# The gate stage of a hybrid GLA and short-convolution layer, computed over pairs of 512-token blocks

## The chip, the cores and the metric

The kernel runs on one core of a Trainium2 chip. Five engines work side by side, each with an instruction queue of its own: PE (TensorE) multiplies matrices, DVE (VectorE) and ACT (ScalarE) work elementwise, POOL (GpSimd) does slower elementwise work and issues DMAs, SP (SyncE) issues DMAs. They meet at semaphores. The metric is the time of one execution in microseconds of device time (us).

## The reference

```python
n   = RMSNorm(h)
z   = n @ W_in
A   : GLA group (chunk-causal state readout, per-head RMSNorm, SiLU gate path)
B   : short gated conv group, SiLU gate path
h   = h + W_out [A ; B]
h   = h + sigmoid(h W_g + b_g) * (p[i] W_ple)
Final RMSNorm.
```

The sequence has 4096 tokens, h has 1024 channels, p has 256, and everything is float32. The change is in the last two lines: the product h W_g (1024x1024), the sigmoid, the small product p W_ple (256x1024), the sum into h, and the final norm over 1024 channels.

## The kernel before

Tokens lie along the free axis in 8 blocks of 512 (TB), channels along the 128 partitions in 8 tiles (KT). The first stage (eight `gla` blocks, to about 645 us) makes the GLA half. Then come 12 steps over pairs of blocks: 8 `conv` steps and 4 `out_proj` steps (g = 0 to 11), about 76.5 us each, and last the gate stage.

Each of these stages multiplies by a scheme with 7 products in place of 8 (P1, P6, P7, P2, P5, P3, P4, in this order, `OPERAND`): the tokens and the channels are halved, a product takes a quadrant (4 tiles of 128 channels by half of the tokens) or a sum or difference of quadrants (t1 to t4), and each product has 4 output tiles q. P1, P6, P7, P4 accumulate in one set of PSUM banks (A), P2, P5, P3 in another (C); between them ACT copies intermediate sums to SBUF (EA, EB). For float32 accuracy every operand is split in a high part (ACT writes XH) and a low part (DVE writes XL), and each tile takes three products: WH XH, WL XH, WH XL. One tile is therefore 4 x 3 = 12 matmuls, one product 48, one round of seven 336.

In the 12 steps a round covers a pair of blocks, so a quadrant has 512 columns. In the gate stage a round covers one block, so a quadrant has 256 columns (HT), and two tiles q share a PSUM bank. There, for each block b, `gate_product` runs the seven products from the weight tile WC, in which all seven weights (2 MB each) lie for the whole stage. The block's h lies in `raw` or `raw_odd`, both operand and residual, and DVE makes t1 to t4 from it (TA, TB_). `ple_unit` makes p W_ple for two tiles at a time, 12 matmuls of 256 columns for each, 96 for a block. `gate_sum` (DVE) adds the PSUM result to a copy, `sigmoid` (ACT) follows, `gate_mix` (DVE, two instructions: multiply by the PSUM result of `ple_unit`, add to the residual), `gate_square` (ACT) squares h, and `add_square` (DVE) sums the squares. The sum over channels is a product with a matrix of ones (`out_stats` on PE), then Ln and Exp on ACT (`out_rms`), and 8 scaled multiplies on DVE (`final_norm`). These engines wait for each other in the order in which each `gate` function lists its calls; there is no scheduler. SP loads the next block's h and p and stores the result; POOL does nothing in the gate stage.

In the 12 steps POOL makes the differences t3 and t1 (L921) and loads the quadrants of the next step into RQ, `block_hi` and `block_lo` split them, and POOL prepares the weights of the next stage, those of the gate too (`strip`, `gate_parts`, `prep_tile`).

## Time and profile before

| what | us |
|---|---|
| three runs | 2001.92, 2003.32, 2003.65 |
| median | 2003.32 |
| span of the profiled execution | 2000.1 |
| gate stage in it, first to last matmul of its rounds | 1569.9 to 1987.6 |
| from there to the end | 12.5 |

The profile holds one execution. Its span is counted from the first instruction to the last; what the device adds around it is not recorded apart, so its own time is known only as this span, which is 3.2 us under the median of the three runs.

### The profile page before, as it was taken

How to read it: one execution, taken by the hardware profiler on the slowest of the kernel's cores; microseconds unless marked ns; L12 is line 12 of the kernel's file. 1: busy time of each engine (PE TensorE's matmuls, PEld its weight loads, DVE VectorE, ACT ScalarE, POOL GpSimd, SP SyncE). 2: the span in 40 equal slices, each digit the busy share in tenths (PEclk: the TensorE clock that was granted, in tenths of full speed). 3: DMA queues.
4: the chain of work that ended last, by engine and by line, in shares of the span. 5: the costliest groups of instructions: out<-in, count | busy, mean ns of one | idle time of the engine just before them, and what ended most of it. 6: DMA issues, size and time to landing. Idle time of an engine off the chain costs nothing.

```text
span 2000.1 us, 28931 instructions
## 1 busy us (share of the span) xinstructions
PE 1973.4 (99%) x11280; PEld 1720.0 (86%) x11280; DVE 1346.4 (67%) x1574; ACT 780.5 (39%) x1221; POOL 692.8 (35%) x758
## 2 busy tenths in 40 slices
PE   6999999999999999999999999999999999999998
PEld 5888888888888888888888888888887999999998
DVE  6766666767644586685685685675575577777776
ACT  5444354444433533232332332323223254455544
POOL 4766656767661132332222221154652000000000
PEclk9999999999999999999999999999999999999999
DMA  6345445354448322237422227585586912222222
GB/s 239 131 167 201 152 161 204 121 194 172 164 163 322 141 95 95 85 107 295 158 88 90 69 95 290 181 301 197 182 301 235 378 68 92 82 87 77 95 96 85
DMA packets 89905, 322.84 MB, mean 161 GB/s; under 512 B 11664, under 2 KB 24384, under 8 KB 78784
## 3 DMA queue, kind: packets, MB, share of 16 engines
q1 hardware_dynamic: 56928, 185.46, 25.5%
q0 software_dynamic: 32864, 135.85, 18.8%
q8 instruction: 74, 1.21, 0.2%
q14 instruction: 39, 0.32, 0.0%
HBM read 193.34 MB, written 127.93 MB: 161 GB/s over the span
## 4 chain that ended last, share of the span: by engine, by line
PE 93%; DVE 3%; issue 1%; ACT 1%; DMA 1%; POOLq 0%; POOL 0%; SPq 0%; DVEq 0%; ACTq 0%
PE bank L1285 14%; PE bank L1291 14%; PE bank L1287 14%; PE bank L994 8%; PE bank L998 8%; PE bank L995 8%; PE bank L1373 5%; PE bank L1371 5%; PE bank L1376 4%; PE bank L1424 2%; PE bank L1423 2%; PE bank L1422 2%; PE bank L1381 1%; PE bank L1119 1%; PE bank L1179 1%
## 5 line engine op out<-in xcount | busy, mean ns | idle before, releaser
L1285 PE MATMUL bank<-XH,WC 128*128 128x512 f32 x1344 | 524.6, 390 | 1.9 <-DVE xt L2285 1.5
L1291 PE MATMUL bank<-XL,WC 128*128 128x512 f32 x1344 | 522.9, 389 | 0.0
L1287 PE MATMUL bank<-XH,WC 128*128 128x512 f32 x1344 | 522.9, 389 | 0.0
L2119 DVE TENSOR_TENSOR XL<-RQ,XH 128x1024 fp32r<-128x1024 f32 x168 | 220.3, 1345 | 218.3 <-ACT XH L1687 216.9
L1285 PEld LDWEIGHTS bank<-XH,WC 128*128 128x128 f32 x1344 | 252.3, 188 | 54.7 <-DVE xt L2285 1.9
L1291 PEld LDWEIGHTS bank<-XL,WC 128*128 128x128 f32 x1344 | 252.3, 188 | 52.5
L1287 PEld LDWEIGHTS bank<-XH,WC 128*128 128x128 f32 x1344 | 252.3, 188 | 51.7
L1373 PE MATMUL bank<-XHg,WC 128*128 128x256 f32 x896 | 246.2, 283 | 0.0
L1371 PE MATMUL bank<-XHg,WC 128*128 128x256 f32 x896 | 246.2, 283 | 0.0
L1687 ACT ACTIVATE XH<-RQ 128x1024 fp32r<-128x1024 f32 x168 | 170.7, 1053 | 168.3 <-PE bank L1291 149.8
L1376 PE MATMUL bank<-XLg,WC 128*128 128x256 f32 x672 | 190.2, 283 | 0.0
L921 POOL TENSOR_TENSOR RQ<-RQ 128x1024 f32<-128x1024 f32 x48 | 116.8, 2456 | 179.3 <-DVE RQ L2138 167.3
L1373 PEld LDWEIGHTS bank<-XHg,WC 128*128 128x128 f32 x896 | 171.9, 192 | 0.4
L1371 PEld LDWEIGHTS bank<-XHg,WC 128*128 128x128 f32 x896 | 171.9, 192 | 0.3
L994 PE MATMUL bank<-XH,QG 128*128 128x512 f32 x384 | 152.5, 397 | 0.0
L998 PE MATMUL bank<-XL,QG 128*128 128x512 f32 x384 | 149.9, 390 | 0.0
L995 PE MATMUL bank<-XH,QG 128*128 128x512 f32 x384 | 149.6, 390 | 0.0
L1376 PEld LDWEIGHTS bank<-XLg,WC 128*128 128x128 f32 x672 | 129.0, 192 | 0.0
L1704 ACT ACTIVATE EA<-bank 128x512 f32<-128x512 f32 x96 | 57.3, 598 | 169.4 <-PE bank L1291 71.2
L766 POOL TENSOR_TENSOR PB<-PB,prep_hi 128x512 f32<-128x512 f32 x84 | 109.8, 1307 | 2.3
L909 POOL DMA_DIRECT2D RQ<-n_scratch x32 | 17.6, 549 | 201.3 <-issue 91.1
L994 PEld LDWEIGHTS bank<-XH,QG 128*128 128x128 f32 x384 | 72.1, 188 | 17.2 <-issue 2.8
(241 smaller groups left out, 3822.8 us busy)
## 6 DMA issues: line engine op xcount, KB each, us to landing
WC<-w_scratch SPq DMA_DIRECT2D x28, 2048.0 KB, 9.8
RQ<-n_scratch POOLq DMA_DIRECT2D x32, 1024.0 KB, 5.4
w_scratch<-prep_hi POOLq DMA_DIRECT2D x84, 256.0 KB, 2.3
w_scratch<-PB POOLq DMA_DIRECT2D x84, 256.0 KB, 2.3
n_scratch<-raw SPq DMA_DIRECT2D x8, 2048.0 KB, 7.3
y_scratch<-y_sb SPq DMA_DIRECT2D x64, 256.0 KB, 2.6
RQ<-y_scratch POOLq DMA_DIRECT2D x16, 1024.0 KB, 7.0
xt<-xb_dram SPq DMA_DIRECT2D x64, 256.0 KB, 4.9
```

The source lines that it names most:

```text
L921: pool.tensor_tensor(RQ[:, a, k], RQ[:, Q22, k], RQ[:, b, k], ALU.subtract).then_inc(made, 1)
L994: nc.tensor.matmul(acc_ap, hh[0], hh[1], start=(k == 0), stop=False)
L995: nc.tensor.matmul(acc_ap, lh[0], lh[1], start=False, stop=False)
L998: mm = nc.tensor.matmul(acc_ap, hl[0], hl[1], start=False, stop=(k == KT - 1))
L1285: nc.tensor.matmul(bank[:], WC[:, i, q, 0, k], xh, start=(k == 0 and i in (P1, P2, P5)), stop=False, skip_group_check=True)
L1287: nc.tensor.matmul(bank[:], WC[:, i, q, 1, k], xh, start=False, stop=False, skip_group_check=True)
L1291: mm = nc.tensor.matmul(bank[:], WC[:, i, q, 0, k], xl, start=False, stop=(k == 3), skip_group_check=True)
L1371: nc.tensor.matmul(acc_ap, WC[:, i, q, 0, k], xh, start=(k == 0 and q % 2 == 0 and i in (P1, P2, P5)), stop=False, skip_group_check=True)
L1373: nc.tensor.matmul(acc_ap, WC[:, i, q, 1, k], xh, start=False, stop=False, skip_group_check=True)
L1376: mm = nc.tensor.matmul(acc_ap, WC[:, i, q, 0, k], XLg[:, z % 2, k], start=False, stop=(k == 3), skip_group_check=True)
L1687: nc.scalar.activation(XH[:, slot(s) + 2 * h:slot(s) + 2 * h + 2], RQ[:, OPERAND[i], 2 * h:2 * h + 2], ACT.Copy).then_inc(sx_hi, 1)
L2119: nc.vector.tensor_tensor(XL[:, k], RQ[:, OPERAND[s % 7], 2 * h:2 * h + 2], XH[:, k].bitcast(F32), ALU.subtract).then_inc(sx_lo, 1)
```

## The change

The gate stage becomes four rounds over pairs of blocks (p = 0 to 3), written as further steps g = 12 to 15 of the same code as `out_proj`: quadrants of 512 columns in RQ, loaded from h_scratch and combined by POOL and DVE, split by `block_hi` and `block_lo` in halves. `product_tile` is one tile q. The pair is finished in 16 units of one tile and one channel tile each (`UNITS`), with 6 matmuls of 512 columns in `ple_unit`. The C sums of the gate use two banks (`C_RING`), the ple results two (`PLE_RING`), one unit per bank.

SBUF is laid out anew. Only three of the seven weight places remain (`RING`); product i is loaded again in every round, once product i-3 is done. The other four places hold the residual tiles (five groups of 1 MB, `res_near` and `res_far`, loaded from h_scratch a second time and stored as the result), p of both blocks, and the weights of `ple_unit`. `add_square` moves from DVE to POOL, the high part of the total (`total_out`) from DVE to ACT, and the sum of squares is kept for 512 tokens at a time, so that each round has two `out_stats` (t = 1, then t = 0), each with 8 `final_norm` instructions.

```diff
+RING = 3
+RES = 5
+PRODUCT = (P2, P5, P3, P4)
+UNITS = tuple([(0, q) for q in range(4)] + [(1, 0), (1, 1), (2, 0), (2, 1), (1, 2), (1, 3), (2, 2), (2, 3)]
+              + [(3, q) for q in range(4)])
+C_RING = (6, 3)
...
+            def stream_weights(p, i):
...
+                sp.wait_ge(sx_free, 4 * (7 * (STEPS + p) + i - RING + 1))
...
+                sp.dma_start(WC[:, gate_place(p, i)].bitcast(F32),
+                             w_scratch[3, i].rearrange("p (q h k c) -> p q h k c", q=4, h=2, k=4)).then_inc(w_chunk[i], 16)
...
+            def gate(p):
+                if p > 0:
+                    load_p(p, 0)
+                    store_out(4 * (p - 1) + 1, 16 * (p - 1) + 4)
+                    store_out(4 * (p - 1) + 2, 16 * (p - 1) + 8)
+                stream_weights(p, P2)
+                if p > 0:
+                    store_out(4 * (p - 1), 16 * (p - 1) + 12)
+                    store_out(4 * (p - 1) + 3, 16 * (p - 1) + 16)
+                stream_weights(p, P5)
+                if p > 0:
+                    load_res(4 * p + 2)
+                    load_res(4 * p + 3)
+                    load_res(4 * p + 1)
+                else:
...
+                load_res(4 * p + 4)
+                stream_weights(p, P3)
+                stream_weights(p, P4)
+                stream_weights(p, 7 + P1)
+                load_p(p + 1, 1)
+                stream_weights(p, 7 + P6)
+                stream_weights(p, 7 + P7)
...
+            def add_square(p, u):
...
+                pool.wait_ge(g_sq, 16 * p + u + 1)
+                if n > 0:
+                    pool.wait_ge(g_acc, n)
+                here = acc[:, RESULT[UNITS[u][0]][0]]
+                pool.tensor_tensor(here, here, square_tile(p, u), ALU.add).then_inc(g_acc, 1)
...
+            for p in range(NP):
+                g = STEPS + p
+                s = 7 * g
+                pool.wait_ge(rq_loaded[Q12], 16 * (g + 1))
+                pool.wait_ge(rq_loaded[Q22], 16 * (g + 1))
+                difference(g, Q12, Q12, t3_made)
+                if p > 0:
+                    add_squares(p - 1, range(8, 16))
+                split_waits(s + P6)
+                pool.wait_ge(t4_made, 2 * (g + 1))
+                difference(g, Q11, Q11, t1_made)
+                if p < NP - 1:
+                    for c in range(8):
+                        pool.wait_ge(rows_stored[c], 16 * 2 * (p + 2))
+                    split_waits(s + P7)
+                    load_quadrant(g + 1, Q12)
+                    split_waits(s + P5)
+                    load_quadrant(g + 1, Q11)
+                add_squares(p, range(4))
+                if p < NP - 1:
+                    split_waits(s + P3)
+                    pool.wait_ge(t1_made, 2 * (g + 1))
+                    load_quadrant(g + 1, Q22)
+                add_squares(p, range(4, 8))
+                if p < NP - 1:
+                    split_waits(s + P4)
+                    load_quadrant(g + 1, Q21)
+            add_squares(NP - 1, range(8, 12))
...
+            def wait_gate_bank(p, i, q):
...
+                elif i == P5 and q < 2:
+                    pe.wait_ge(g_sum, sums_to(p, 0, q + 2))
+                elif i == P5:
+                    pe.wait_ge(g_sum, sums_to(p, 2, q - 2))
+                else:
+                    pe.wait_ge(g_sum, sums_to(p, 1, q))
...
-            def gate(b):
-                gate_product(b, P1)
-                gate_product(b, P6)
-                if b > 0:
-                    out_stats(b - 1)
-                gate_product(b, P7)
-                for c, i in enumerate((P2, P5, P3)):
-                    gate_product(b, i)
-                    ple_unit(b, 2 * c)
-                    ple_unit(b, 2 * c + 1)
-                if b < NB - 1:
-                    gate_product(b, P4)
-                ple_unit(b, 6)
-                ple_unit(b, 7)
-                if b == NB - 1:
-                    gate_product(b, P4)
...
+            def out_stats(p, t):
+                n = 2 * p + 1 - t
+                pe.wait_ge(out_split, n + 1)
+                pe.wait_ge(g_sum, 12 * (p + 1))
+                mean_of_split(C_RING[1 - t], total_hi[:], total_lo[:]).then_inc(out_mean, 1)
...
+            def gate(p):
+                g = STEPS + p
+                def with_ple(c, q):
+                    product_tile(g, PRODUCT[c], q, None)
+                    ple_unit(p, c, q)
+                stage_of(g, P1, None)
+                product_tile(g, P6, 0, None)
+                if p > 0:
+                    out_stats(p - 1, 0)
+                for q in range(1, 4):
+                    product_tile(g, P6, q, None)
+                stage_of(g, P7, None)
+                for q in range(4):
+                    with_ple(0, q)
+                for two in range(2):
+                    for c in (1, 2):
+                        with_ple(c, 2 * two)
+                        with_ple(c, 2 * two + 1)
+                if p < NP - 1:
+                    for q in range(3):
+                        with_ple(3, q)
+                    out_stats(p, 1)
+                    with_ple(3, 3)
+                    return
+                ple_unit(p, 3, 0)
+                ple_unit(p, 3, 1)
+                product_tile(g, P4, 0, None)
+                product_tile(g, P4, 1, None)
+                out_stats(p, 1)
+                ple_unit(p, 3, 2)
+                product_tile(g, P4, 2, None)
+                ple_unit(p, 3, 3)
+                product_tile(g, P4, 3, None)
+                last_stats()
...
+            def total_out(p, t):
+                act.wait_ge(g_acc, added_to(p, 2 if t == 1 else 3))
...
+                nc.scalar.activation(total_hi[:], acc[:, t], ACT.Copy).then_inc(out_sum_hi, 1)
...
+            def gate(p):
...
+                if p > 0:
+                    sigmoid(p - 1, 15)
+                block_hi(s + 1)
+                if p > 0:
+                    gate_square(p - 1, 14)
+                copy_sum(g, P1, 0)
+                if p > 0:
+                    gate_square(p - 1, 15)
+                copy_sum(g, P1, 1)
+                if p > 0:
...
+                    out_rms(p - 1, 1)
+                copy_sum(g, P1, 2)
+                copy_sum(g, P1, 3)
+                block_hi(s + 2)
+                if p > 0:
+                    total_out(p - 1, 0)
+                copy_sum(g, P6, 0)
+                copy_sum(g, P6, 1)
+                if p > 0:
+                    out_rms(p - 1, 0)
+                copy_sum(g, P6, 2)
+                copy_sum(g, P6, 3)
+                block_hi(s + 3)
+                split_p_hi(p, 0)
+                split_p_hi(p, 1)
+                block_hi(s + 4)
+                for q in range(4):
+                    sigmoid(p, q)
+                    copy_sum(g, P7, q)
+                    if q > 0:
+                        gate_square(p, q - 1)
+                block_hi(s + 5)
+                gate_square(p, 3)
+                for u in range(4, 12):
+                    sigmoid(p, u)
+                    if u == 9:
+                        block_hi(s + 6)
+                    if u > 4:
+                        gate_square(p, u - 1)
+                block_hi(s + 7)
+                if p < NP - 1:
+                    sigmoid(p, 12)
+                    gate_square(p, 11)
+                    sigmoid(p, 13)
+                    total_out(p, 1)
...
+            def total_split(p, t):
+                dve.wait_ge(out_sum_hi, 2 * p + 2 - t)
+                nc.vector.tensor_tensor(total_lo[:], acc[:, t], total_hi[:].bitcast(F32), ALU.subtract).then_inc(
...
+            def gate(p):
...
+                else:
+                    gate_mix(p - 1, 14)
+                    block_lo(s + 1)
+                    gate_mix(p - 1, 15)
+                    final_norm(p - 1, 1)
+                block_lo(s + 2)
+                if p > 0:
+                    total_split(p - 1, 0)
+                    final_norm(p - 1, 0)
+                block_lo(s + 3)
+                make_t4(g)
+                split_p_lo(p, 0)
+                split_p_lo(p, 1)
+                block_lo(s + 4)
+                gate_sum(p, 0)
+                for u in range(1, 4):
+                    gate_sum(p, u)
+                    gate_mix(p, u - 1)
+                block_lo(s + 5)
+                gate_mix(p, 3)
+                gate_sum(p, 4)
+                for u in range(5, 12):
+                    gate_sum(p, u)
+                    if u == 9:
+                        block_lo(s + 6)
+                    gate_mix(p, u - 1)
+                block_lo(s + 7)
+                gate_mix(p, 11)
+                make_t2(g + 1)
+                if p < NP - 1:
+                    gate_mix(p, 12)
+                    total_split(p, 1)
+                    gate_mix(p, 13)
```

Three places in the order of instructions. The first is DVE where one round ends and the next begins. Before (one block to the next), with XLg the low part, acc and total the sum of squares, L2461 the final norm:

```order
L2392 TENSOR_TENSOR acc<-acc,osq 128x512 x2
L2400 TENSOR_TENSOR total<-acc 128x512
L2403 CAST total_hi<-total 128x512
L2405 TENSOR_TENSOR total_lo<-total,total_hi 128x512
L2358 TENSOR_TENSOR XLg<-TB__108,XHg 128x1024
L2358 TENSOR_TENSOR XLg<-TA,XHg 128x1024
L2349 TENSOR_TENSOR TA<-raw_odd,TB__108 128x1024
L2351 TENSOR_TENSOR TB__108<-raw_odd,TB__108 128x1024
L2358 TENSOR_TENSOR XLg<-raw_odd,XHg 128x1024
L2321 TENSOR_TENSOR PL<-p_raw,PH 128x1024
L2461 SCALAR_TENSOR_TENSOR raw<-raw,vec,R_out 128x512 x4
```

The same place now, with L2196 `block_lo`, L2413 and L2418 `gate_mix`, L2433 `final_norm`, L2423 `total_split`, L2215 `make_t4`, L2391 `split_p_lo`:

```order
L2196 TENSOR_TENSOR XL<-RQ,XH 128x1024 x2
L2413 TENSOR_TENSOR gt<-gt,bank 128x512
L2418 TENSOR_TENSOR res_near<-res_near,gt 128x512
L2433 SCALAR_TENSOR_TENSOR res_near<-res_near,vec,R_out 128x512 x8
L2196 TENSOR_TENSOR XL<-RQ,XH 128x1024 x2
L2423 TENSOR_TENSOR total_lo<-acc,total_hi 128x512
L2433 SCALAR_TENSOR_TENSOR res_near<-res_near,vec,R_out 128x512 x8
L2196 TENSOR_TENSOR XL<-RQ,XH 128x1024 x2
L2215 TENSOR_TENSOR RQ<-RQ 128x1024 x2
L2391 TENSOR_TENSOR PL<-p_raw,PH 128x1024 x2
```

Before, the low part of the total was made ahead of everything of the next block; now that of t = 0 stands behind eight norms of t = 1 and one `block_lo`.

The second place is ACT at the same point of the program now, with L1794 `copy_sum`, L1771 `block_hi`, L1901 and L1904 `out_rms`, L1894 `total_out`, L1887 `gate_square`:

```order
L1887 ACTIVATE osq<-res_near 128x512
L1794 ACTIVATE EA<-bank 128x512
L1925 ACT_TABLE_LOAD
L1901 ACTIVATE R_out<-bank,eps 128x512
L1904 ACTIVATE R_out<-R_out 128x512
L1794 ACTIVATE EA<-bank 128x512 x2
L1771 ACTIVATE XH<-RQ 128x1024 x2
L1894 ACTIVATE total_hi<-acc 128x512
L1794 ACTIVATE EB<-bank 128x512 x2
L1901 ACTIVATE R_out<-bank,eps 128x512
L1904 ACTIVATE R_out<-R_out 128x512
```

The high part of the t = 0 total stands behind all four copies of P1 and the high part of P7's operand.

The third place is DVE at units 9 to 11 of a round, where L2404 is `gate_sum`:

```order
L2404 TENSOR_TENSOR gt<-bank,EA 128x512
L2196 TENSOR_TENSOR XL<-RQ,XH 128x1024 x2
L2413 TENSOR_TENSOR gt<-gt,bank 128x512
L2418 TENSOR_TENSOR res_near<-res_near,gt 128x512
L2404 TENSOR_TENSOR gt<-bank,EB 128x512
L2413 TENSOR_TENSOR gt<-gt,bank 128x512
```

The low part of P4's operand (L2196) stands between the sum of unit 9 and the mix of unit 8, and the mix of unit 8 is what frees the PSUM bank for the `ple_unit` of unit 10.

## Rows read from the trace of the kernel before

**Rows 1.** The page: busy time, share of the span and instructions of each engine.
```profile
PE 1973.4 (99%) x11280; PEld 1720.0 (86%) x11280; DVE 1346.4 (67%) x1574; ACT 780.5 (39%) x1221; POOL 692.8 (35%) x758
```

**Rows 2.** Windows of the gate stage and of the end: length, busy by engine, clock, DMA.
```profile
1569.60:1987.60 418.00, 418.00 (x3472) 417.30 (x3471) 303.89 (x393) 206.93 (x328) 0.00 (x0) 1.00 0.28 106
1987.60:2000.10 12.50, 4.04 (x19) 2.92 (x17) 7.80 (x18) 4.77 (x9) 0.00 (x0) 0.83 0.51 168
```

**Rows 3.** Waits of PE from 640 to 1572: total, times, longest.
```profile
PE bank L1285 <- DVE xt L2285: 1.5, 1, 1.5
```

**Rows 4.** Timeline of PE: start, duration (us); matmuls of 512 columns, then of 256.
```profile
1289.99 0.39 PE L1285 MATMUL bank<-XH,WC 128*128 128x512 f32 x1
...
1299.51 0.39 PE L1285 MATMUL bank<-XH,WC 128*128 128x512 f32 x1
...
1702.08 0.28 PE L1376 MATMUL bank<-XLg,WC 128*128 128x256 f32 x1
...
1705.68 0.28 PE L1376 MATMUL bank<-XLg,WC 128*128 128x256 f32 x1
```

**Rows 5.** Timeline of PE and ACT where the first tile of a P1 ends.
```profile
1342.35 0.39 PE L1285 MATMUL bank<-XH,WC 128*128 128x512 f32 x1
...
1342.55 0.60 ACT L1704 ACTIVATE EA<-bank 128x512 f32<-128x512 f32 x1 [1.60 <-PE bank L1291]
```

**Rows 6.** Timeline of DVE: low parts, final norms, the first instruction of a mix.
```profile
1363.16 2.36 DVE L2119 TENSOR_TENSOR XL<-RQ,XH 128x1024 fp32r<-128x1024 f32 x2 [7.26 <-ACT XH L1687]
...
1642.45 2.73 DVE L2461 SCALAR_TENSOR_TENSOR raw<-raw,vec,R_out 128x512 f32<-128x512 f32 x4
...
1597.38 0.68 DVE L2379 TENSOR_TENSOR gt<-gt,bank 128x512 f32<-128x512 f32 x1
```

**Rows 7.** ACT: a timeline row of two high parts, then groups with mean ns.
```profile
1351.20 2.00 ACT L1687 ACTIVATE XH<-RQ 128x1024 fp32r<-128x1024 f32 x2
...
L1837 ACT ACTIVATE osq<-raw 128x512 f32<-128x512 f32 x24 | 15.2, 632 | 16.6 <-DVE raw L2383 16.6
...
L1850 ACT ACT_TABLE_LOAD x7 | 9.0, 1283 | 0.1
...
L1898 ACT ACTIVATE R_out<-bank,eps 128x512 f32<-128x512 f32 x7 | 4.8, 689 | 0.1
```

**Rows 8.** Timeline of DVE and POOL, 1397 to 1407, and one more POOL row.
```profile
1397.10 1.29 DVE L2273 TENSOR_TENSOR xt<-xt,EB 128x512 f32<-128x512 f32 x2
1399.46 5.17 DVE L2273 TENSOR_TENSOR xt<-xt,EB 128x512 f32<-128x512 f32 x2 [1.07 <-DMA xt<-xb_dram]
1404.55 2.47 DVE L2285 TENSOR_TENSOR xt<-xt,bank 128x512 f32<-128x512 f32 x4
...
1398.88 5.20 POOL L921 TENSOR_TENSOR RQ<-RQ 128x1024 f32<-128x1024 f32 x2 [0.60 <-DMA RQ<-y_scratch]
...
1360.93 1.30 POOL L766 TENSOR_TENSOR PB_late<-PB_late,hi_late 128x512 f32<-128x512 f32 x1
```

**Rows 9.** Timeline of SP and DVE in the last `out_proj` step (L511 weights of the gate).
```profile
1522.69 2.41 SPq L511 DMA_DIRECT2D WC<-w_scratch  x3
...
1545.39 0.69 DVE L2273 TENSOR_TENSOR xt<-xt,EA 128x512 f32<-128x512 f32 x1 [3.80 <-DMA xt<-xb_dram]
```

**Rows 10.** The end: matmuls with ones, last norms, a window where the clock changes.
```profile
1987.75 1.89 PE L1460 MATMUL bank<-acc,ones 128*128 128x256 f32 x8
...
1991.60 1.13 PE L1460 MATMUL bank<-osq,ones 128*128 128x256 f32 x4 [1.09 <-ACT osq L1837]
...
1991.06 6.42 DVE L2455 SCALAR_TENSOR_TENSOR raw_odd<-raw_odd,vec,R_out 128x256 f32<-128x256 f32 x16 [0.82 <-ACT R_out L1893]
...
1995.00:1996.00 1.00, 0.00 (x0) 0.00 (x0) 1.00 (x4) 0.00 (x0) 0.00 (x0) 0.95 1.00 327
```

**Rows 11.** The page's DMA issues (KB each, us to landing), and a busy window.
```profile
WC<-w_scratch SPq DMA_DIRECT2D x28, 2048.0 KB, 9.8
...
1530.00:1535.00 5.00, 5.00 (x23) 4.13 (x22) 3.80 (x7) 1.79 (x3) 0.00 (x0) 1.00 1.00 423
```

More of the change, by code:

```diff
@@ new lines, in product_tile @@
+                for k in range(4):
+                    if q == 0 and k % 2 == 0:
+                        pe.wait_ge(sx_hi, 2 * s + k // 2 + 1)
+                    xh, xl = XH[:, slot(s) + k], XL[:, slot(s) + k]
+                    nc.tensor.matmul(bank[:], WC[:, weights_of, q, 0, k], xh, start=(k == 0 and i in (P1, P2, P5)),
+                                     stop=False, skip_group_check=True)
+                    nc.tensor.matmul(bank[:], WC[:, weights_of, q, 1, k], xh, start=False, stop=False,
+                                     skip_group_check=True)
+                    if q == 0 and k % 2 == 0:
+                        pe.wait_ge(sx_lo, 2 * s + k // 2 + 1)
+                    mm = nc.tensor.matmul(bank[:], WC[:, weights_of, q, 0, k], xl, start=False, stop=(k == 3),
+                                          skip_group_check=True)
+                    if q == 3:
+                        mm.then_inc(sx_free, 1)
+                    elif k == 3:
+                        mm.then_inc(product_done, 1)
+                    if hook is not None:
+                        hook(16 * i + 4 * q + k)
@@ L1404, in ple_unit, with ple_tile @@
-            def ple_unit(b, u):
-                n = 8 * b + u
+            def ple_tile(t, m, acc_ap, tokens):
+                for k in range(PLE_K):
+                    nc.tensor.matmul(acc_ap, WPH[:, k, m], PH[:, t, k, tokens], start=(k == 0), stop=False)
+                    nc.tensor.matmul(acc_ap, WPL[:, k, m], PH[:, t, k, tokens], start=False, stop=False)
+                    mm = nc.tensor.matmul(acc_ap, WPH[:, k, m], PL[:, t, k, tokens], start=False,
+                                          stop=(k == PLE_K - 1))
+                return mm
@@ L1445, in out_stats @@
[L1445 to L1471 removed]
+                pe.wait_ge(p_lo, 2 * p + t + 1)
@@ L1478, in _ @@
                 step(g)
-            for b in range(NB):
-                gate(b)
-            last_stats()
+            for p in range(NP):
+                gate(p)
         @block.scalar
@@ L1943, in _ @@
                 step(g)
-            for b in range(NB):
-                gate(b)
+            for p in range(NP):
+                gate(p)
         @block.vector
@@ L2370, in gate_sum @@
-                other = EBg if u >= 4 else EAg
-                dve.wait_ge(g_copied, 6 * b + (1, 5, 3)[u // 2] + pair)
-                nc.vector.tensor_tensor(gt[:, n % 3], ps[GATE_C[pair]][:], other[:, pair], ALU.add).then_inc(g_sum, 1)
-            def gate_mix(b, u):
-                n = 8 * b + u
+                if n == 0:
+                    for c_ in range(8):
+                        dve.wait_ge(rows_stored[c_], 16 * 2 * NP)
+                wait_product(dve, 7 * g + PRODUCT[c], q)
+                dve.wait_ge(e_copied, 12 * g + (0, 8, 4)[c] + q + 1)
@@ L2450, in last_norm @@
[L2450 to L2463 removed]
+                wait_res(dve, p, c)
@@ L2517, in _ @@
                 out_proj(g)
-            for b in range(NB):
-                gate(b)
-            for n, t in enumerate((1, 0)):
-                dve.wait_ge(out_rstd, NB + n)
-                last_norm(t)
+            for p in range(NP):
+                gate(p)
 def kernel(x, p, norm_w, w_in, w_alpha_up, b_alpha, gla_norm_w, conv_w, conv_b,
```

714 lines of the change are left out of this document (263 added, 451 removed).

## The prediction

> **What bounds the kernel now.** I read the page first, and in it the busy shares: PE is busy for 99% of the span [rows 1]. Then the windows of the stages: in the gate stage PE is busy for all of its 418.0 us at clock 1.00, DVE for 303.9, ACT for 206.9, POOL for none [rows 2]. Then the waits of PE: between 640 and 1572 there is one of note, 1.5 us, for a DVE sum [rows 3]. So PE's own stream sets the time, and a change counts by how long PE takes for its matmuls and by each wait that it brings. The timeline of PE gives the price of a matmul, by the distance of their starts, since they overlap: 42 of 512 columns in 9.52 us, 0.2267 each; 30 of 256 columns in 3.60 us, 0.120 each [rows 4]. Two short ones cost 0.240, so 0.0133 us are paid for every pair that could be one.
>
> **PE's own work.** Before, a block has 336 + 96 matmuls of 256 columns, eight blocks 3456, with 14 of 512 columns for the statistics; that is 414.7 + 3.2 = 417.9 us, which is the 418.0 of the window. After, a round has 336 + 96 of 512 columns, four rounds 1728, or 391.7 us, and the statistics still take 7 x 2 matmuls. Gain: 23.0 us. Of the removed work on DVE (the sums of squares, the total) nothing counts by itself, as PE never waited for it.
>
> **The last step before the gate.** All three first weights of the gate, 6 MB, were issued together at 1522.7, because SP first waited for POOL's preparation of the ple weights; the xt tiles came late behind them (DVE waits 3.8 us for one), and that is where PE's 1.5 us lie [rows 3, 9]. Now this wait stands behind P4, the three loads go out one by one, and the 3 MB of residuals only after P5. I take the 1.5 us as gained.
>
> **The boundary of two rounds.** Let 0 be the start of P1 in a round p > 0. A tile takes 12 x 0.227 = 2.72 us, a product 10.88, a `ple_unit` 1.36, a unit 4.08, a statistic 0.45. PE comes to `out_stats(p-1, 0)` after P1 and one tile of P6, at 13.60. It waits for `total_split`. The chain behind it:
> - ACT sees a tile 0.2 us after PE has ended it [rows 5]. Copy P1 q1 runs 5.64 to 6.24 (0.60), then the table load of 1.28, Ln 0.69 and Exp, taken like the square of its size, 0.63 [rows 5, 7]: R_out for t = 1 at 8.9.
> - DVE then does eight norms at 0.68 (four in 2.73), to 14.3, and `block_lo` for P7, 2.36, to 16.7 [rows 6].
> - On ACT the copies of P1 end at 11.7, `block_hi` for P7 takes 2.0 to 13.7, `total_out` 0.6 to 14.3 [rows 5, 7]. It is there before DVE wants it.
> - `total_split` is one DVE instruction, about 0.65: done at 17.3, seen by PE at 17.4.
>
> So PE stands 3.8 us at each of three boundaries, 11.4 us. The floor is ACT's side alone, 14.3 + 0.7 = 15.0, or 1.4 a boundary. Queued behind it on PE are the rest of P6 and P7, and all engines wait for those. What is late next: Ln and Exp for t = 0 at about 22.8, eight norms to 28.2, `block_lo` for P2 to 30.5, `make_t4` to 32.8, while P2 starts at 36.9 (13.6 + 3.8 + 0.45 + 3 x 2.72 + 10.88); POOL's difference t1 (two of 2.4 to 2.6) to 38, P5's parts to 41.3, the first gate sum 41.9. PE's third tile of P2 wants that at 45.1. No further stall.
>
> **The low part inside unit 9.** Let 0 be the end of the product tile of unit 9. PE has 1.36 + 2.72 us of work and then wants the bank that the mix of unit 8 frees, at 4.08. DVE's sum ends at 0.9, ACT's sigmoid at 1.6 (one of 512 like the square, 0.63), its two high parts at 2.65 and 3.6, DVE's low parts at 3.9 and 4.85, the multiply of the mix at 5.5 (0.68; a whole mix is two such instructions, 1.36 at most) [rows 6, 7]. A stall of 1.5 us in each of four rounds, 6.0 us.
>
> **POOL beside DVE.** POOL was idle in this stage; now each round has four differences and 14 additions. At 1399 two DVE additions that read SBUF twice took 5.17 us instead of 1.29, as long as POOL's two differences beside them (5.20), while four that read a PSUM bank took 2.47 beside POOL, as ever [rows 8]. So the second instruction of a mix, the low parts and `make_t2` can each wait for a POOL instruction (1.30 for an addition, 2.6 for a difference), the sums and norms hardly. Where this falls between units it is hidden by 2 us of slack in a unit (4.08 against 0.68 + 1.36 on DVE). After unit 9 it is not: POOL gets P4's parts at 4.9, then does two differences to 10.4 and three late additions, while DVE has two mixes, the low part of the next P1, a mix and `make_t2`. Without contention `ple_unit` 13 has its bank 1.4 us early; with every one of these in the way I get 0.7 us late there and 0.7 at `ple_unit` 14, in three rounds. Bounds 0 and 4.5 us (8 if also the low parts in unit 3 are caught); I take 3.0, nearer the bound with contention, since the row shows full blocking. The Trainium skill (SBUF — State Buffer, Who interferes with whom) says that an instruction with two SBUF inputs and a GpSimd one that reads SBUF exclude each other, and that the first to start keeps the port for its whole length. By this rule the cost is the 4.5 and not less; the trace agrees with the exclusion, not surely with who wins.
>
> **The end.** Let E be the end of the last P4 tile. DVE has four norms of t = 1 until E + 1.6, the last mix until E + 2.9, ACT the square until E + 3.6. A matmul with ones in plain float32 is long: the eight records of 256 columns take 1.73 us from first to last start plus one, two for each matmul, so one of 512 columns takes 0.86 [rows 10]. Then Ln and Exp to E + 6.2, eight norms to E + 11.7, and the store about 2.6 (2000.1 less 1997.5) with its issue: E + 14.7 against 12.5 now [rows 2, 10]. Loss 2.2, and 0.3 for the ple units that stand before P4 in the last round.
>
> **Sum.** -23.0 - 1.5 + 11.4 + 6.0 + 3.0 + 2.2 + 0.3 = -1.6 us: a span of 1998.5 for 2000.1. The median of the runs stands 3.2 above the span, so 2001.7 us. That is inside the 0.2% (4 us) which a measurement of this kernel can tell from no change.
>
> **Edits costed at nothing.** The weights that are now reloaded: a product has two products' time, 21.8 us, and an issue lands in 9.8 [rows 11]. The tightest is P3: SP issues it after the norms of t = 0, the stores, P5 and the four residual loads. From 28.3 about 6 MB stand in the queue, P3 and two quadrants make 10; at the 0.42 MB per us of the busy window [rows 11] they are in at about 53, and P3 starts at 61.4. Without this cover each us more is a us of PE, three or four times. RQ, p and the residuals come earlier than this relative to use.
>
> **Rivals.**
> 1. *The waits are smaller and the gain stays* (faster). For it: PE waits almost nowhere now, and DVE and POOL have 27% or more idle in the stage. Against: the boundary chain has no slack in it. With the boundary at its floor of 1.4, contention 0 and the rest as above, 2003.3 - 23 - 1.5 + 4.2 + 6 + 2.5 = 1991.5; with no stall at all 1981.
> 2. *The clock drops at the boundaries* (slower). In the tail PE's last matmul ends at 1992.7, and the clock is 1.00 until about 1995.9, then 0.5, 1.2 GHz: the window 1995 to 1996 has 0.95 [rows 10]. It fell 3.2 us after PE's last work, and I foresee 3.8 us of idleness three times. From there each matmul costs up to double until the clock is back; bounds per drop are 0 and, if it lasts as long as the fall took, 2 to 3 us of PE time, so up to 9: 2011. The point from which it decides is a stall of about 3 us. The Trainium skill (TensorE: Matmul & The Clock Gate, Part 1) says that the throttled state is the default and activity releases it; by this rule a drop follows where the idleness is long enough; the trace agrees in its tail, and shows no wait of that length inside the stage.
> 3. *Weights or residuals late* (slower). If the queue moves at 0.25 MB per us, P3 comes at 28 + 40 = 68, 7 us late in three rounds: 2023. Against: the busy window moved 423 GB/s [rows 11].
> 4. *The matmuls of the new rounds are not at 0.227*. All 12 steps run the same code at this pace, so I leave it 1 in 50, within the range.
>
> **How the numbers follow.** The forecast, a net within 4 us, has 0.42. Rival 1 and sums below -4 have 0.32: the boundary or the contention need only be 2.4 us less than I say. Rival 2 0.12, rival 3 and stalls that I have not found 0.14. The likeliest case alone spans 1999.3 to 2007.3. For 8 in 10 I go down to 1991, rival 1, and up to 2011, rival 2. Faster by over 0.2% 0.33, within 0.42, slower 0.25.
>
> **What the profile after would show.** 3456 fewer matmuls of 256 columns and 1728 of 512 at 0.227; three PE waits of about 3.8 us on total_lo at the second tile of P6; four of 1.5 on gt before the ple matmuls of unit 10; smaller ones at units 13 and 14; the wait at 1546 gone; the last matmul of P4 14.7 before the end. I am wrong if DVE gets to `total_split` well before 17, if the clock shows 0.5 inside the stage, or if PE waits for a WC transfer.

## The result, and the profile after

The changed kernel takes 2015.1 us (median of 4 runs, 2012.4 to 2020.1) against 2003.5 for the kernel before (4 runs): ratio 1.0064, 95% interval 1.0053 to 1.0076. It is slower by 0.6%, clear of the noise, and outside the predicted range. Its profiled execution took 2013.6 us, its span is 2011.8 us where 1998.5 was forecast: 13.3 us to explain.

The page of the changed kernel, its busy line, answers to [rows 1]:

```profile
PE 1961.7 (98%) x9546; PEld 1632.0 (81%) x9546; DVE 1321.8 (66%) x1490; ACT 766.7 (38%) x1156; POOL 816.0 (41%) x842
```

1734 PE instructions are gone, the 1728 foreseen and six in the tail, and 512 columns still take 0.2267 us at full clock, yet the span is longer: the share of PE fell below 99%. So the waits come next. PE's waits from 1400 to 2030 (total, times, longest), which answer to [rows 3]:

```profile
PE bank L1115 <- DVE total_lo L2423: 10.5, 3, 3.5
PE bank L1485 <- DVE gt L2413: 9.0, 11, 1.6
PE bank L1390 <- DVE xt L2362: 3.4, 1, 3.4
```

The first two rows are the boundary (forecast 11.4) and units 9 to 14 (forecast 6.0 + 3.0). The third should have gone; it has more than doubled. The timeline of PE (start, duration) shows what waits do not:

```profile
1540.09 0.79 PE L1390 MATMUL bank<-XH,WC 128*128 128x512 f32 x1 [3.41 <-DVE xt L2362]
1540.68 0.63 PE L1392 MATMUL bank<-XH,WC 128*128 128x512 f32 x1
1541.11 0.63 PE L1396 MATMUL bank<-XL,WC 128*128 128x512 f32 x1
...
1694.45 0.50 PE L1115 MATMUL bank<-total_hi,ones 128*128 128x512 f32 x1 [3.49 <-DVE total_lo L2423]
1694.79 0.39 PE L1116 MATMUL bank<-total_lo,ones 128*128 128x512 f32 x1
...
1696.32 0.63 PE L1396 MATMUL bank<-XL,WC 128*128 128x512 f32 x1
1696.75 0.63 PE L1390 MATMUL bank<-XH,WC 128*128 128x512 f32 x1
...
1699.59 0.40 PE L1392 MATMUL bank<-XH,WC 128*128 128x512 f32 x1
```

Behind a wait of 3.4 or 3.5 us the starts stand 0.43 us apart instead of 0.23. That is the pace of half the clock, 1.2 GHz instead of 2.4. The windows (length, busy by engine, granted clock, DMA) say the same: two boundaries show it, the third does not. A clock of 0.5 inside the stage was one of the prediction's signs of being wrong.

```profile
1694.00:1700.00 6.00, 5.55 (x17) 4.43 (x18) 0.39 (x1) 0.45 (x1) 0.00 (x0) 0.72 1.05 395
1700.00:1706.00 6.00, 6.00 (x28) 4.91 (x28) 4.58 (x7) 2.91 (x6) 0.00 (x0) 1.00 0.22 94
1801.00:1806.00 5.00, 4.05 (x11) 3.23 (x12) 0.90 (x2) 0.00 (x0) 0.00 (x0) 0.66 1.03 369
1909.00:1915.00 6.00, 5.66 (x25) 4.71 (x26) 0.57 (x2) 1.81 (x3) 0.00 (x0) 1.00 1.01 380
```

The loss is read off the starts: 17 intervals from 1694.45 to 1700.06 take 5.61 us, 3.85 at 0.2267, so 1.8 us at a boundary where the clock fell; from 1540.09 to 1545.80 it is 5.71 for 13, so 2.8 us.

Why the wait for xt grew is read from what stands ahead of it: VectorE's low part of P5, which wants GpSimd's difference t1 (L971). Timelines of POOL, DVE and SP, changed kernel:

```profile
1515.79 0.56 POOL L913 DMA_DIRECT2D tile_raw<-w_ple_dram  x1 [7.23 <-DMA g_scratch<-tile_raw]
1524.52 1.04 POOL L915 TENSOR_SCALAR tile_hi<-tile_raw 128x1024 fp32r<-128x1024 f32 x1 [8.17 <-DMA tile_raw<-w_ple_dram]
...
1529.93 4.75 POOL L971 TENSOR_TENSOR RQ<-RQ 128x1024 f32<-128x1024 f32 x2
...
1533.46 3.57 DVE L2196 TENSOR_TENSOR XL<-RQ,XH 128x1024 fp32r<-128x1024 f32 x2 [12.29 <-ACT XH L1771]
...
1504.07 22.08 SPq L515 DMA_DIRECT2D WC<-w_scratch  x3
```

and of POOL in the kernel before, the same instructions:

```profile
1510.10 0.56 POOL L863 DMA_DIRECT2D tile_raw<-w_ple_dram  x1 [2.76 <-DMA g_scratch<-tile_raw]
1513.94 1.05 POOL L865 TENSOR_SCALAR tile_hi<-tile_raw 128x1024 fp32r<-128x1024 f32 x1 [3.28 <-DMA tile_raw<-w_ple_dram]
...
1522.49 4.75 POOL L921 TENSOR_TENSOR RQ<-RQ 128x1024 f32<-128x1024 f32 x2 [2.67 <-DVE RQ L2138]
```

SP now issues the gate's weights from 1504, not at 1522.7 [rows 9], while GpSimd prepares its two ple tiles one after the other. GpSimd's DMA waits grow from 2.76 and 3.28 us to 7.23 and 8.17, and t1, queued behind the second tile, starts 7.4 us later. That is the theory for the first miss; for the second it is that the falls of the clock follow from PE's idleness. The experiments test both, and the terms that held.

### The profile page after: what moved, and what is told of

Read it like the earlier page. It is cut to its first block, busy times and chain, and to the rows that moved or that the text cites. A ratio compares the mean times of both kernels' runs of the same rounds, so it can differ in the third digit from the quotient of the medians.

```text
span 2011.8 us, 25501 instructions
## 1 busy us (share of the span) xinstructions
PE 1961.7 (98%) x9546; PEld 1632.0 (81%) x9546; DVE 1321.8 (66%) x1490; ACT 766.7 (38%) x1156; POOL 816.0 (41%) x842
## 4 chain that ended last, share of the span: by engine, by line
PE 87%; DVE 6%; ACT 2%; issue 2%; DMA 2%; POOL 1%; DVEq 0%; SPq 0%; ACTq 0%; POOLq 0%
PE bank L1390 18%; PE bank L1396 18%; PE bank L1392 18%; PE bank L1088 8%; PE bank L1092 8%; PE bank L1089 8%; PE bank L1485 1%; DVE XL L2196 1%; PE bank L1487 1%; PE bank L1486 1%; PE bank L1213 1%; DVE res_near L2433 1%; PE bank L1273 1%; DVE XL L2030 1%; PE bank L1264 1%
## 5 line engine op out<-in xcount | busy, mean ns | idle before, releaser
L1390 PE MATMUL bank<-XH,WC 128*128 128x512 f32 x1792 | 701.1, 391 | 3.5 <-DVE xt L2362 3.4
L1392 PE MATMUL bank<-XH,WC 128*128 128x512 f32 x1792 | 699.3, 390 | 0.0
L1396 PE MATMUL bank<-XL,WC 128*128 128x512 f32 x1792 | 699.2, 390 | 0.0
L2196 DVE TENSOR_TENSOR XL<-RQ,XH 128x1024 fp32r<-128x1024 f32 x224 | 292.9, 1342 | 280.2 <-ACT XH L1771 278.7
L1390 PEld LDWEIGHTS bank<-XH,WC 128*128 128x128 f32 x1792 | 337.9, 189 | 74.2 <-DVE xt L2362 3.8
L1396 PEld LDWEIGHTS bank<-XL,WC 128*128 128x128 f32 x1792 | 337.6, 188 | 70.6
L1392 PEld LDWEIGHTS bank<-XH,WC 128*128 128x128 f32 x1792 | 337.8, 188 | 69.7
L1771 ACT ACTIVATE XH<-RQ 128x1024 fp32r<-128x1024 f32 x224 | 227.4, 1053 | 225.1 <-PE bank L1396 175.8
L971 POOL TENSOR_TENSOR RQ<-RQ 128x1024 f32<-128x1024 f32 x64 | 164.1, 2586 | 295.0 <-DVE RQ L2215 283.5
L1794 ACT ACTIVATE EA<-bank 128x512 f32<-128x512 f32 x128 | 76.1, 595 | 185.3 <-PE bank L1396 89.1
L1027 POOL TENSOR_TENSOR acc<-acc,osq 128x512 f32<-128x512 f32 x52 | 72.6, 1396 | 154.3 <-ACT osq L1887 153.3
L804 POOL TENSOR_TENSOR PB<-PB 128x512 f32<-128x512 f32 x48 | 63.3, 1319 | 64.3 <-issue 58.7
L1088 PEld LDWEIGHTS bank<-XH,QG 128*128 128x128 f32 x384 | 72.1, 188 | 17.2 <-issue 2.8
L1092 PEld LDWEIGHTS bank<-XL,QG 128*128 128x128 f32 x384 | 72.1, 188 | 15.8
L1089 PEld LDWEIGHTS bank<-XH,QG 128*128 128x128 f32 x384 | 72.2, 188 | 14.6
L1794 ACT ACTIVATE EB<-bank 128x512 f32<-128x512 f32 x64 | 38.2, 598 | 114.1 <-PE bank L1396 114.1
L1088 PE MATMUL bank<-VH,XH 128*128 128x512 f32 x192 | 76.8, 400 | 0.0
```

The lines of the kernel that those rows point to most:

```text
L971: pool.tensor_tensor(RQ[:, a, k], RQ[:, Q22, k], RQ[:, b, k], ALU.subtract).then_inc(made, 1)
L1027: pool.tensor_tensor(here, here, square_tile(p, u), ALU.add).then_inc(g_acc, 1)
L1088: nc.tensor.matmul(acc_ap, hh[0], hh[1], start=(k == 0), stop=False)
L1089: nc.tensor.matmul(acc_ap, lh[0], lh[1], start=False, stop=False)
L1092: mm = nc.tensor.matmul(acc_ap, hl[0], hl[1], start=False, stop=(k == KT - 1))
L1390: nc.tensor.matmul(bank[:], WC[:, weights_of, q, 0, k], xh, start=(k == 0 and i in (P1, P2, P5)), stop=False, skip_group_check=True)
```

## The experiments

All times are medians beside runs of the kernel before on the same chip (2002.7 to 2004.0).

**The last step, 1: early weights in the kernel before.** SP's wait for GpSimd's tiles is moved behind three weight loads and four stores, and the small load of p goes with it; nothing else changes.

```diff
-                if g == STEPS - 1:
-                    sp.wait_ge(tile_stored, 16 * 2 * (STRIPS + PLE_K))
-                    sp.dma_start(p_raw[:], pb[0]).then_inc(p_loaded, 16)
                 next_weights(g, P1)
...
+                if g == STEPS - 1:
+                    sp.wait_ge(tile_stored, 16 * 2 * (STRIPS + PLE_K))
+                    sp.dma_start(p_raw[:], pb[0]).then_inc(p_loaded, 16)
```

> The kernel before, with one edit: in the last output-projection step SP no longer waits for GpSimd's two ple tiles ahead of the three weight loads, so these go out early, one by one, as in the changed kernel. Theory (early weight loads slow GpSimd's ple preparation, t1 and P5's operand come late, TensorE waits and its clock falls): TensorE's wait in that step grows from 1.5 to about 3.4 us and the clock falls once, some 4.6 us more in all, 2008. Rival (the wait hangs on the xt tiles that queue behind 6 MB of weights, as the prediction had it): the wait goes, 2002.

2008.1 us, ratio 1.0020 (1.0011 to 1.0030). Timelines of POOL and PE:

```profile
1525.80 1.05 POOL L865 TENSOR_SCALAR tile_hi<-tile_raw 128x1024 fp32r<-128x1024 f32 x1 [7.26 <-DMA tile_raw<-w_ple_dram]
...
1531.22 4.76 POOL L921 TENSOR_TENSOR RQ<-RQ 128x1024 f32<-128x1024 f32 x2
...
1541.39 0.50 PE L1285 MATMUL bank<-XH,WC 128*128 128x512 f32 x1 [2.82 <-DVE xt L2285]
```

The edit alone brings GpSimd's longer DMA waits and the late t1, in a kernel with none of the new gate. The wait is 2.8 us, not the 3.4 expected, and no fall of the clock follows it. The profiled span is 4.3 us longer than before, but only 1.3 of that is this wait: 2.9 lie before 1500, where the edit changes nothing. The mechanism is shown by the rows; the size of the median's rise is not accounted for by them.

**2: the wait put back in the changed kernel.**

```diff
+                if g == STEPS - 1:
+                    sp.wait_ge(tile_stored, 16 * 2 * (STRIPS + PLE_K))
                 next_weights(g, P1)
...
-                sp.wait_ge(tile_stored, 16 * 2 * (STRIPS + PLE_K))
```

> The changed kernel, with one thing put back: SyncE waits for the stores of GpSimd's two per-layer tiles ahead of the gate's first weight loads, as before the change. Theory (these loads, 22 us of DMA each, slow GpSimd's own small loads and stores and so make its t1 difference 7.4 us late): the wait for xt in the last step before the gate goes from 3.4 us back to about 1.5, and the granted clock does not fall behind it (2.7 us in the profile): 4.6 us less, 2010.5. Rival (another part of the change makes t1 late): wait and clock as in the changed kernel, 2015.

2016.7 us, 1.0074 (1.0058 to 1.0089): a miss, the same as the changed kernel within the intervals. Timelines:

```profile
1524.03 4.75 POOL L972 TENSOR_TENSOR RQ<-RQ 128x1024 f32<-128x1024 f32 x2 [3.82 <-DVE RQ L2216]
...
1549.48 0.69 DVE L2351 TENSOR_TENSOR xt<-xt,EA 128x512 f32<-128x512 f32 x1 [5.46 <-DMA xt<-xb_dram]
...
1553.09 0.79 PE L1391 MATMUL bank<-XH,WC 128*128 128x512 f32 x1 [4.15 <-DVE xt L2363]
```

t1 is timely again, but now the xt tile of [rows 9] itself is late, by 5.46 us where it was 3.80. A second cause stood behind the first.

**3: also GpSimd's new loads later.** The changed kernel loads the gate's operands here (in run 2, 1 MB at 1528.7 and 1 MB at 1531.8), which the kernel before did not. Run 2's edit stays in, and both loads are moved.

```diff
+                if g < STEPS - 1:
-                load_quadrant(g + 1, Q12)
+                    load_quadrant(g + 1, Q12)
...
                 split_waits(s + P3)
+                if g == STEPS - 1:
+                    load_quadrant(g + 1, Q12)
+                    load_quadrant(g + 1, Q11)
```

> The changed kernel with SyncE's wait put back ahead of the weight loads (which made t1 timely, but left TensorE waiting 4.15 us for an xt tile whose load VectorE awaited for 5.5 us), and with GpSimd's first two loads of the gate's operands, 2 MB from 1528.7 and 1531.8, moved behind P3's parts, some 12 us. Theory (these loads, which the change adds in this stretch, hold up the xt loads): the wait for xt goes back to 1.5 us or less and the clock stays, 2.7 + 2.4 us less than with the wait alone: about 2011. Rival (the xt loads are late behind the three weight loads alone): the wait stays at about 4 us, 2016.

2011.2 us, 1.0037 (1.0023 to 1.0051). PE has no wait left in this stretch; the window (length, busy by engine, clock, DMA):

```profile
1540.00:1570.00 30.00, 30.00 (x134) 24.86 (x133) 21.40 (x23) 6.74 (x7) 7.41 (x6) 1.00 0.94 344
```

So the wait for xt had two causes, both of them DMA traffic that the change puts there; the second rests on one profile of each run. The Trainium skill (DMA: Bandwidth & Descriptors, Issuing engines are not separate DMA queues) says that DMAs of the sync and gpsimd engines run on the same 16 DMA engines and interleave; the slower loads here agree.

**4 and 5: t1 ahead of the tiles.** In run 4 both tiles stand behind the load of Q11, in run 5 only the second, behind t1. The edit of run 5:

```diff
-                    for n in range(PLE_K):
-                        prep_tile(n)
+                    prep_tile(0)
                 split_waits(s + P6)
                 pool.wait_ge(t4_made, 2 * (g + 1))
                 difference(g, Q11, Q11, t1_made)
+                if g == STEPS - 1:
+                    prep_tile(1)
```

> The changed kernel, with GpSimd's two ple tiles prepared after the difference t1 and the loads of Q12 and Q11 instead of ahead of them. Theory: the 3.4 us wait at P5 of the last output-projection step goes and with it 2.7 us at half clock, so about 6 us less, 2009. Rival (xt tiles or the weights' traffic itself hold P5): the wait stays, same time as the changed kernel, 2015.

Run 4: 2031.4 us, 1.0144 (1.0127 to 1.0161), a miss. Its PE waits, and POOL and ACT:

```profile
PE bank L1390 <- issue: 18.3, 1, 18.3
...
1570.49 1.16 POOL L959 DMA_DIRECT2D RQ<-h_scratch  x2
1581.10 4.63 POOL L971 TENSOR_TENSOR RQ<-RQ 128x1024 f32<-128x1024 f32 x2 [9.45 <-DMA RQ<-h_scratch]
...
1586.85 2.19 ACT L1771 ACTIVATE XH<-RQ 128x1024 fp32r<-128x1024 f32 x2 [26.24 <-DVE RQ L2207]
```

The wait for xt is gone, but the tiles hold the next two loads in GpSimd's queue to 1570.5, and 18.3 us of PE are lost at the gate's start. (The next expectation blames SyncE's queue for it; these rows show that it was GpSimd's.)

> The changed kernel, with GpSimd's second per-layer tile prepared behind its t1 difference instead of ahead of it; weights are loaded as in the changed kernel. Theory (t1 is late because that tile stands ahead of it): t1 is made before 1525 us instead of 1534.6, the wait for xt goes altogether with its clock fall, 6.5 us less than the changed kernel: 2008.5. Rival (the tile's stores, now later, hold SyncE's queue ahead of the gate's P2 weights, as happened when both tiles stood behind the Q11 load and cost 18.3 us): slower than 2015.

Run 5: 2010.0 us, 1.0039 (1.0024 to 1.0055): no wait for xt, 5.1 us less than the changed kernel for 6.5 expected, with the weights early all the same.

Six profiles have the weights early and both tiles ahead of t1: the changed kernel, run 1, and four runs further down whose edits lie in the gate. How late t1 starts, counted from the start of VectorE's low part two ahead of P5's (1505.66 in the changed kernel), gives PE's wait each time:

| profile | t1's start, us | PE's wait for xt, us |
|---|---|---|
| `after_fill` | 24.53 | 3.68 |
| changed kernel | 24.27 | 3.41 |
| `after_stats_later` | 23.99 | 3.14 |
| `after_small_adds` | 23.89 | 3.04 |
| `before_weights_early` | 23.67 | 2.82 |
| `after_unit9_swap` | 21.43 | 0.59 |

The wait is the first number less 20.85, to 0.01 us in all six; before the change the first number was 17.88. So the late t1 is this wait, and its size varies from run to run with GpSimd's loads (6.56 us in `after_unit9_swap` for the 8.17 of the second tile).

**The boundary: statistics two tiles later.**

```diff
-                product_tile(g, P6, 0, None)
+                for q in range(3):
+                    product_tile(g, P6, q, None)
                 if p > 0:
                     out_stats(p - 1, 0)
-                for q in range(1, 4):
-                    product_tile(g, P6, q, None)
+                product_tile(g, P6, 3, None)
```

> The changed kernel, with the t = 0 statistic on TensorE after the third tile of P6 instead of the first, 5.4 us later. Theory: the chain of norm, low part and split ends 3.7 us after the old place, so all three waits go (11 us) and with them the falls of the clock inside the stage (1.7 us each, two in the profile): 14 us less, 2001. Rival 1 (the later statistic moves the second norm and P2's operand past P2's start): a new wait of 1 to 3 us a round before P2. Rival 2 (the falls of the clock do not hang on these waits): 11 us less, and the clock still falls.

1998.3 us (10 runs, 1994.7 to 2000.9), 0.9972 (0.9962 to 0.9981): faster than the kernel before. The waits:

```profile
PE bank L1485 <- DVE gt L2413: 9.0, 11, 1.6
PE bank L1390 <- DVE xt L2362: 3.1, 1, 3.1
```

The 10.5 us are gone and not replaced, and the clock is 1.00 at all boundaries. The two profiled spans differ by 15.0 us, of which 10.5 are waits, 0.5 the restarts behind them and 3.6 clock. The medians differ by 16.8; the changed kernel's other runs lie up to 6.5 us above the profiled one.

**The boundary: the same wait, filled.** The delay is left, only the idleness is taken away.

```diff
+FILL = 15
...
+                pe.wait_ge(g_sum, 12 * (p + 1))
+                if t == 0:
+                    for _ in range(FILL):
+                        nc.tensor.matmul(ps[C_RING[1]][:], ones[:], XH[:, slot(7 * (STEPS + p + 1) + P6)], start=True,
+                                         stop=True)
                 pe.wait_ge(out_split, n + 1)
-                pe.wait_ge(g_sum, 12 * (p + 1))
```

> The changed kernel, with 15 matmuls of 512 columns that nobody reads ahead of TensorE's wait for the first statistics of a pair (3 times), 15 x 0.2267 = 3.4 us: the wait of 3.5 us is filled with work, and nothing else is moved, so that the statistics come no earlier. Theory (TensorE's idling of 3.5 us makes the clock fall behind it): no half-clock stretch behind the three boundaries, 3.4 us less than the profiled changed kernel and up to 6 less than its slower runs: about 2011. Rival (the falls come from something else, or the waits themselves are all of the cost): 2015.

2011.7 us, 1.0038 (1.0027 to 1.0049), 3.5 less than the changed kernel. Windows at two boundaries, which answer to those above:

```profile
1696.00:1702.00 6.00, 5.97 (x26) 4.97 (x27) 0.58 (x1) 1.81 (x3) 0.00 (x0) 1.00 1.02 389
1797.00:1803.00 6.00, 5.90 (x27) 4.55 (x26) 4.83 (x6) 2.20 (x4) 0.00 (x0) 1.00 1.03 366
```

The statistics come no earlier, and the clock does not fall at any of the three boundaries. One profile could be luck here, as run 2 shows. But the mean granted clock of the whole execution is 0.997 or 0.998 in all seven runs of this kernel, and 0.994, 0.994, 0.995 and 0.997 in the four of the changed kernel: the fall belongs to the idleness. The Trainium skill (TensorE: Matmul & The Clock Gate, Part 1) says that activity releases the throttle; these windows agree.

**Unit 9, 1: the low part behind the mix.**

```diff
-                    if u == 9:
-                        block_lo(s + 6)
                     gate_mix(p, u - 1)
+                    if u == 9:
+                        block_lo(s + 6)
```

> The changed kernel, with the low part of P4's operand after the mix of unit 8 instead of ahead of it, on VectorE. Theory: the wait of 1.55 us (1.7 with the refill) in each of four rounds goes, 7 us less, 2008, and P4's operand is still there in time. Rival (contention or GpSimd's differences, which now start 1.4 us later, bring it back at units 12 to 14): under 3 us less, with waits at those units grown.

2018.6 us, 1.0079 (1.0063 to 1.0096): a miss, no better than the changed kernel. Timelines of DVE (the sum of unit 9 first), POOL and PE:

```profile
1643.86 0.69 DVE L2404 TENSOR_TENSOR gt<-bank,EA 128x512 f32<-128x512 f32 x1 [2.07 <-PE bank L1396]
...
1649.88 6.57 DVE L2418 TENSOR_TENSOR res_near<-res_near,gt 128x512 f32<-128x512 f32 x1
...
1649.90 4.76 POOL L971 TENSOR_TENSOR RQ<-RQ 128x1024 f32<-128x1024 f32 x2
1654.61 1.28 POOL L1027 TENSOR_TENSOR acc<-acc,osq 128x512 f32<-128x512 f32 x1
...
1657.80 0.47 PE L1485 MATMUL bank<-PH,WPH 128*128 128x512 f32 x1 [1.79 <-DVE gt L2413]
1664.03 0.70 PE L1485 MATMUL bank<-PH,WPH 128*128 128x512 f32 x1 [1.91 <-DVE gt L2413]
```

And in the changed kernel, the same instructions of DVE and POOL:

```profile
1647.86 0.69 DVE L2404 TENSOR_TENSOR gt<-bank,EA 128x512 f32<-128x512 f32 x1 [2.07 <-PE bank L1396]
...
1655.21 1.67 DVE L2418 TENSOR_TENSOR res_near<-res_near,gt 128x512 f32<-128x512 f32 x1
...
1653.89 5.25 POOL L971 TENSOR_TENSOR RQ<-RQ 128x1024 f32<-128x1024 f32 x2
```

Counted from the sum of unit 9, GpSimd's t3 differences start at 6.0 us in both kernels: the swap does not move them, since the low part waits for ACT's high part and starts at 2.4 in both (1646.29 and 1650.29). What moves is VectorE's addition of unit 9, which reads SBUF twice: from 7.35 to 6.02, onto the start of the differences. It took 6.57 us instead of 0.69, since two differences and an addition of GpSimd's in a row went ahead of it. In the last round, which has no t3 after it, the swap did take the 1.55 us away.

**Unit 9, 2: in the last round only,** with the two other edits that helped (statistics after the third tile, second ple tile behind t1).

> The changed kernel with three edits: the first statistics of a pair behind the third tile of P6, GpSimd's second per-layer tile behind its t1 difference, and in the last round alone VectorE's low part of unit 9 behind the mix of unit 8. Theory: 1998.3 of the first edit alone, less 3.1 + 0.4 of the wait for xt and 1.5 of clock behind it, less 1.7 for one unit 10: about 1991.5. Rival (the wait for xt is replaced by a later one in the same step, and the unit's gain goes elsewhere): 1996 to 2000.

1993.7 us (5 runs, 1992.4 to 1994.4), 0.9954 (0.9940 to 0.9967): the fastest kernel of this study, 21.4 us below the changed kernel. PE's waits:

```profile
PE bank L1486 <- DVE gt L2414: 7.5, 10, 1.6
PE bank L1391 <- issue: 0.5, 1, 0.5
```

The waits for xt and for the statistics are gone, and one of the four of unit 9.

**Unit 9, 3: in all rounds, with t3 behind three additions,** on top of those edits.

```diff
+                if p > 0:
+                    add_squares(p - 1, range(8, 11))
                 difference(g, Q12, Q12, t3_made)
                 if p > 0:
-                    add_squares(p - 1, range(8, 16))
+                    add_squares(p - 1, range(11, 16))
```

> The kernel with three edits, with VectorE's low part of unit 9 behind the mix of unit 8 in all four rounds and GpSimd's additions of units 8 to 10 ahead of its t3 difference. Theory (the swap alone gained nothing since VectorE's addition of unit 9 began with GpSimd's two t3 differences and an addition back to back and took 6.6 us): with the differences off that place the waits of 1.55 us in unit 10 go in three more rounds, 3 x 1.7 = 5 us less than 1993.7: 1988.5. Rival (the 5 us of differences meet another addition of VectorE's, one in each unit): a wait of 2 to 4 us in each round, 1993 to 2000.

1995.4 us, 0.9958 (0.9946 to 0.9970): no gain over `after_three`, as the rival said. Timelines of POOL and DVE:

```profile
1655.39 6.71 POOL L971 TENSOR_TENSOR RQ<-RQ 128x1024 f32<-128x1024 f32 x2
...
1655.05 4.81 DVE L2199 TENSOR_TENSOR XL<-RQ,XH 128x1024 fp32r<-128x1024 f32 x2 [1.65 <-ACT XH L1774]
...
1662.58 3.44 DVE L2210 TENSOR_TENSOR RQ<-RQ 128x1024 f32<-128x1024 f32 x2
```

The differences now meet the next low part (2.36 alone [rows 6], here 4.81), and PE waits 1.3 to 1.5 and 1.8 us in two other places, in three rounds.

**GpSimd's additions, 8 of 512 columns** (the sum of squares leaves out most of its terms).

```diff
-                pool.tensor_tensor(here, here, square_tile(p, u), ALU.add).then_inc(g_acc, 1)
+                pool.tensor_tensor(here[:, 0:8], here[:, 0:8], square_tile(p, u)[:, 0:8], ALU.add).then_inc(g_acc, 1)
```

> The changed kernel, with GpSimd's additions of squares cut to 8 of 512 columns, so that the sum of squares leaves out most of its terms; number and order of instructions stay. Theory (the additions meet VectorE's instructions that read and write SBUF alone): the waits of units 13 and 14 (2.8 us in three rounds, with 7 refills of 0.16) mostly go, 2012. Rival (they come from VectorE's low part and GpSimd's differences, not from the additions): waits stay, 2015. The waits of 3.5 us ahead of the statistics and of 1.55 us in unit 10 stay in both.

2010.5 us, 1.0035 (1.0023 to 1.0047). In its waits the second row is now

```profile
PE bank L1485 <- DVE gt L2413: 6.4, 5, 1.6
```

The six waits of units 13 and 14, 2.6 us, are gone. The other 0.2 of the forecast's contention is one wait in the last round, which stays. So the price of moving the squares' sum to GpSimd is 2.6 us and six restarts; the differences alone do not make it.

## Why the prediction was wrong

**The step that failed: "I take the 1.5 us as gained"** (the last step before the gate). The wait was put down to the three weight loads issued together, and their move forward was costed as a relief only. What they are moved past was not asked. The runs showed two prices: they slow GpSimd's small DMAs, so that t1 is 7.4 us late (the six profiles of the table, run 5), and the changed kernel's own operand loads delay the xt tiles (runs 2 and 3). In the profile the wait is 1.9 us longer instead of 1.5 shorter, and 2.8 us of half clock follow it: +4.7 for -1.5.

**The term left out of the sum: rival 2.** It was described rightly, with its threshold ("a stall of about 3 us") below the forecast stall of 3.8, and then given 0.12 and no share of the sum. Its price was 1.7 and 1.8 us for the two falls of the profile, inside its bounds of 0 and 3. A fall followed 15 of the 21 boundary waits of 3.5 us in the seven profiles that have them idle (none of three in run 2). What decides in which is not shown. The 15 cost 1.4 to 3.0 us each, 2.0 on average, so some 1.4 us per boundary belonged in the sum. (A half-clock stretch as long as the fall's 3.2 us loses 1.6 us, not the 2 to 3 that the prediction worked out.)

The whole account of the profiled span, in us against the kernel before:

| term | forecast | measured |
|---|---|---|
| PE's work | -23.0 | -23.0 (a round's 434 matmuls at 0.2267) |
| last step before the gate | -1.5 | +1.9 wait, +2.8 clock |
| boundary waits | +11.4 | +10.5 |
| unit 9 | +6.0 | +6.2 (4 x 1.55) |
| VectorE beside GpSimd | +3.0 | +2.8 |
| restart after each of the 14 waits in the gate | 0 | +2.3 (0.16 each: a wait of 1.55 makes a gap of 1.94 where 0.23 is due) |
| clock at the boundaries | 0 | +3.6 |
| tail, and ple units ahead of P4 | +2.5 | +2.3 |
| stages before 1500 | 0 | +1.1 |
| not assigned | | +1.2 |
| sum | -1.6 | +11.7 |

**What held.** The boundary chain was right to 0.3 us per wait, with its place and its releaser; `after_stats_later` shows that no later wait hid behind it, as the text said. Unit 9's 1.5 us was 1.55. The contention, 3.0, was 2.8, and `after_small_adds` shows the source of 2.6 of it; its parts at `ple_unit` 13 and 14 are 0.5 to 0.6 and 0.33 to 0.36, where 0.7 and 0.7 were the worst case. (Three rounds of these make 4.2, not the 4.5 of the text.) The tail is 14.8 for 14.7. No streamed weight or residual was late (rival 3: PE has no wait for a DMA in the stage), and the matmuls kept their pace at full clock (rival 4). The 1.1 us before 1500 lie in stages that the change does not touch, and are no cost of it: VectorE's low part that starts at 1504.6 before and 1505.7 in the changed kernel starts as late as 1508.2 in run 3. The 1.2 were not traced. Against such shifts of 1 to 4 us, the waits and clock rows of a profile are firmer than its span.

## What to carry to other kernels

When a load is issued earlier, price what it is moved beside: the small DMAs of other engines, and what is queued behind those. Before counting a wait as gained, name what is late next, here twice in the same step. A forecast wait of over 3 us on TensorE carries a clock term in the sum; two tiles more of cover at the boundary turned the change from 1.006 into 0.997. Taking a wait out of an engine's stream moves all that stands behind it, and in unit 9 an addition moved by 1.3 us collided with another engine's work that stayed where it was.

## What the runs showed of the hardware

- The clock did not fall at once: at 1694.45 TensorE resumed at full pace, was at half from 1695.9 to 1699.3, and was full again. Waits of 3.0 to 4.2 us had such a stretch of 2.1 to 5.6 us behind them mostly; one of 2.82 us had none. In `three_unit9_all` a half-clock stretch of 3.4 us also came behind waits of 1.3 and 1.8 us, 6 us apart.
- A VectorE instruction with two SBUF inputs can lose to several GpSimd ones in a row: 6.57 us for 0.69. The Trainium skill (SBUF — State Buffer, Who interferes with whom) says that whoever issues first keeps the port for its whole instruction. The exclusion agrees with this row. Who was first can't be told from it, as the two starts are 0.02 us apart (0.10 in the next round, GpSimd first, and 6.44 us), and the rule gives no reason for VectorE missing both hand-overs between GpSimd's three. In the changed kernel VectorE's addition started 1.3 us into the first of the same two differences and was done in 1.67 us, so it got in between them.
- Four executions of the changed kernel spread over 7.7 us, five of `after_three`, which has no boundary or xt waits, over 2.1; six of `three_unit9_all`, with its waits of 1.3 and 1.8 us, over 4.9.
